# S5 stage of a two-layer decoder kernel: layer norm inside the turning matmuls, 32-row state matmuls side by side, feature-major readout, late row normalising

## The reference, cut to what matters

```python
h = _layernorm(DEEPNORM_ALPHA * h + _swiglu(...) + ple, ln2_g[0], ln2_b[0])     # layer 0 ends
...
bu = jnp.einsum('bsgc,gpc->bsgp', u, B_bar)            # u = h in 128 groups of 16 channels, 64 complex states each
_, states = lax.associative_scan(combine, (a, bu), axis=1)   # x[t] = A_bar * x[t-1] + bu[t]
y = jnp.einsum('bsgp,gcp->bsgc', states, C_mat).real.reshape(B, S, D)
y = y + d_skip * h
z = jax.nn.gelu(y)
val, gate = jnp.split(z @ w_glu, 2, axis=-1)
mix = val * jax.nn.sigmoid(gate)
...
h = _layernorm(DEEPNORM_ALPHA * h + mix, ln1_g[1], ln1_b[1])
```

## Time and profile before

| | us |
|---|---|
| median of 3 runs | 2477.44 (2476.77 to 2480.57) |
| the profiled execution | 2475.3 |
| span of the profiled execution, first to last instruction | 2473.5 |
| PE busy over the span | 2339.3 (95%) |
| first MATMUL of the S5 stage (L580) | at 1276.5 |
| first MATMUL of glu (L352) | at 1430.1 |

### The profile page before, as it was taken

The page is one execution under the profiler, slowest core; times in us unless marked ns, Lnnn a source line. Parts: engine busy times, 40 slices in busy tenths (PEclk is TensorE's granted clock), DMA queues, the critical chain, the costliest instruction groups (busy, mean ns, idle before and its releaser), DMA issues.

```text
span 2473.5 us, 32913 instructions
## 1 busy us (share of the span) xinstructions
PE 2339.3 (95%) x10996; PEld 1926.3 (78%) x10996; DVE 1456.8 (59%) x1906; ACT 1033.1 (42%) x1134; POOL 245.7 (10%) x345
## 2 busy tenths in 40 slices
PE   8999899999999999999948499989999999999996
PEld 6888687888888888888835488778888888888885
DVE  5544757666667776557846755475455444444555
ACT  4443544444444334443333054344444443344432
POOL 0000038501111011101230000010000000000001
PEclk9998999999999999999969799999999999999998
DMA  6554254767787667757684156556555565555553
GB/s 236 184 182 127 89 198 144 234 223 257 257 266 251 226 231 242 238 195 256 226 203 162 51 183 195 170 187 195 189 189 191 187 190 194 194 188 188 190 191 111
DMA packets 136991, 483.01 MB, mean 195 GB/s; under 512 B 18656, under 2 KB 19168, under 8 KB 135744
## 3 DMA queue, kind: packets, MB, share of 16 engines
q1 hardware_dynamic: 121568, 429.44, 53.5%
q0 software_dynamic: 14048, 50.80, 6.7%
q10 hardware_dynamic: 1280, 1.48, 0.2%
HBM read 457.80 MB, written 19.14 MB: 193 GB/s over the span
## 4 chain that ended last, share of the span: by engine, by line
PE 91%; DVE 5%; DMA 2%; issue 1%; ACT 1%; DVEq 0%; SPq 0%; ACTq 0%
PE ps L352 28%; PE ps L354 28%; PE ps L353 28%; PE ps L592 1%; PE ps L368 1%; PE ps L631 1%; DVE res L1205 1%; DMA raw<-in_w_in 1%; DVE w_lo L977 1%; DVE gated L1547 1%; DVE res L1207 1%; DMA h_quarter<-res 1%; DVE gated L1545 1%; DMA raw<-in_w_glu 0%; ACT w_hi L692 0%
## 5 line engine op out<-in xcount | busy, mean ns | idle before, releaser
L977 DVE TENSOR_TENSOR w_lo<-raw,w_hi 128x1024 fp32r<-128x1024 f32 (+1 forms) x782 | 953.5, 1222 | 861.3 <-ACT w_hi L692 855.4
L692 ACT ACTIVATE w_hi<-raw 128x1024 fp32r<-128x1024 f32 (+1 forms) x782 | 822.1, 1053 | 1190.0 <-PE ps L354 1157.9
L352 PE MATMUL ps<-w_hi,x_hi 128*128 128x512 f32 (+1 forms) x2336 | 917.3, 393 | 17.8 <-DVE x_lo L985 14.2
L354 PE MATMUL ps<-w_hi,x_lo 128*128 128x512 f32 (+1 forms) x2336 | 911.2, 390 | 0.0
L353 PE MATMUL ps<-w_lo,x_hi 128*128 128x512 f32 (+1 forms) x2336 | 910.8, 390 | 0.0
L352 PEld LDWEIGHTS ps<-w_hi,x_hi 128*128 128x128 f32 x2336 | 443.0, 190 | 109.5 <-DVE x_lo L985 16.1
L354 PEld LDWEIGHTS ps<-w_hi,x_lo 128*128 128x128 f32 x2336 | 442.9, 190 | 91.5
L353 PEld LDWEIGHTS ps<-w_lo,x_hi 128*128 128x128 f32 x2336 | 443.2, 190 | 88.6
L352 PE MATMUL ps<-w_hi,hid_hi 128*128 128x512 f32 x704 | 275.2, 391 | 0.0
L353 PE MATMUL ps<-w_lo,hid_hi 128*128 128x512 f32 x704 | 274.1, 389 | 0.0
L354 PE MATMUL ps<-w_hi,hid_lo 128*128 128x512 f32 x704 | 274.0, 389 | 0.0
(11 more groups left out here) (201 smaller groups left out, 1378.6 us busy)
## 6 DMA issues: line engine op xcount, KB each, us to landing
raw<-in_w_inA SPq DMA_DIRECT2D x192, 512.0 KB, 4.2
raw<-in_w_inB SPq DMA_DIRECT2D x160, 512.0 KB, 4.2
raw<-in_w_outA SPq DMA_DIRECT2D x96, 512.0 KB, 4.3
raw<-in_w_outB SPq DMA_DIRECT2D x80, 512.0 KB, 4.3
raw<-in_w_in SPq DMA_DIRECT2D x64, 512.0 KB, 4.0
raw<-in_w_gate SPq DMA_DIRECT2D x64, 512.0 KB, 4.3
raw<-in_w_glu SPq DMA_DIRECT2D x64, 512.0 KB, 4.2
raw<-in_w_out SPq DMA_DIRECT2D x32, 512.0 KB, 4.3
```

The source lines that it names most:

```text
L352: pe.matmul(o, hi[:, kt + k, cols], WH[:, s, k, 0:width], start=(kt + k == 0), stop=False)
L354: last = pe.matmul(o, lo[:, kt + k, cols], WH[:, s, k, 0:width], start=False, stop=(kt + k == depth - 1))
L692: act.activation(WH[:, s, :, 0:width], RAW[:, s, :, 0:width], ACT.Copy).then_inc(hi_ready, 1)
L977: dve.tensor_tensor(WL[:, s, :, 0:width], RAW[:, s, :, 0:width], WH[:, s, :, 0:width].bitcast(F32), ALU.subtract).then_inc(lo_ready, 1)
```

## The change

It touches the S5 stage, what is laid ready for it, and the normalising of RES.

- DVE makes two scaled and step-permuted identities: DQ (1/sigma of each token on the diagonal) and DC (-mean/sigma). PE multiplies RES, not yet normalised, by DQ: this turns tokens x features to features x tokens and applies 1/sigma. ONES times DC gives the shift. ACT makes gain and bias of it (CG), DVE adds both while copying to UT. The SBUF copies, `by_pairs`, U4, the Toeplitz table and POOL's clearing and 16 DMAs go.
- Input: 32 rows (a) of a feature tile against a 32 x 128 table, 32 matmuls a tile with 64 moving columns, straight into states-on-partitions form; the transposes back and e_slots go. Each of the four a has its own PSUM bank.
- Response in the block: 16 matmuls a tile of 32 x 32, row group a to column group a, started when half 0 of the scan has done 44 steps.
- Readout: 32 matmuls a tile, K = 128, 32 stationary columns of the table, the states (every 128th element of ST) moving, 64 columns; output features x tokens, so GELU goes to Z and straight to XH and XL without transposes.
- Scan: `lag` 9 in place of 17.
- Eight input tables are loaded during `outB0`, eight behind the first glu chunks; 16 slots in place of 10; glu chunks 4 to 7 behind the readout tables.
- RES is normalised by DVE alone during glu (`norm_late`, 16 instructions); `load_gb(2)` waits for it.
- `input_matrix` takes B without its fourfold copy, loaded in 8 smaller DMAs in place of 5.

```diff
+            def out_with_tables():
+                nb, per, c0, _ = PHASES["outB0"]
+                for j in range(nb * per):
+                    load(t["w_outB0"], j, c0 + j, 0, None, WB)
+                    if j == RING:
+                        sp.wait_ge(w_used, c0)
+                        sp.wait_ge(e_stored[0], 16 * 11)
+                        sp.wait_ge(e_stored[1], 16 * 5)
+                    if j >= 8 and j % 4 == 0:
+                        input_table(j // 4 - 2)
...
-                glu_chunks(RING, 2 * RING - 1)
-                sp.wait_ge(w_used, PHASES["glu"][2])
-                for q4 in range(4):
-                    quarter_normed(sp, 4 + q4 + 1)
...
-                        sp.dma_start(HQ[q4 % 2][32 * q:32 * q + 32, :, :], RES[:, q, cols]).then_inc(h4_in[q4 % 2], 16)
...
+                for tile in range(8, KT):
                     input_table(tile)
                 for n in range(KT):
+                    sp.wait_ge(e_done, n + 1)
+                    sp.dma_start(TS[n][:], c_dram[tile_of(n)].rearrange("p (a c n) -> p a c n", a=4, c=2)).then_inc(ts_in[n], 16)
+                glu_chunks(RING, 2 * RING)
...
+            def turn_u(kt):
+                for q in range(TT):
+                    last = pe.matmul(by_step(kt // 2 % 7, kt % 2, q), RES[:, q, P * tile_of(kt):P * (tile_of(kt) + 1)],
+                                     DQ[:, q, :].rearrange("p (s n) -> p s n", s=SUB), start=True, stop=True)
...
+            pe.wait_ge(u_ready, KT)
+            for kt in range(KT):
+                pe.wait_ge(ts_in[kt], 16)
...
+                for ri in range(2):
+                    for s in range(SUB):
+                        for a in range(4):
+                            rows = slice(PW * a, PW * (a + 1))
+                            last = pe.matmul(PS[:, 4 * (kt % 2) + a, SLOTS * ri:SLOTS * (ri + 1)], TS[kt][rows, s, ri, :],
+                                             UT[rows, kt, s, :], start=(s == 0), stop=(s == SUB - 1))
+                last.then_inc(e_done, 1)
...
+            pe.wait_ge(scan[0], 3 * 44)
+            for kt in range(KT):
+                for lag in range(SUB):
                     for a in range(4):
...
+                        pe.matmul(outputs(kt, a, lag, SUB), KTAB[rows, tile_of(kt), lag, :],
+                                  UT[rows, kt, 0:SUB - lag, :].rearrange("p s n -> p (s n)"),
+                                  start=(kt % 2 == 0 and lag == 0), stop=False, skip_group_check=True)
+            def read_out(kt):
+                pe.wait_ge(ts_in[kt], 32)
+                for s in range(SUB):
                     for ri in range(2):
+                        for a in range(4):
+                            last = pe.matmul(outputs(kt, a, s, s + 1), TS[kt][:, a, ri, PW * s:PW * (s + 1)],
+                                             ST[:, :, ri, 4 * kt + a], start=False, stop=(ri == 1), skip_group_check=True)
                 last.then_inc(y_done, 1)
...
+                act.activation(CG[:, kt % 2], PS[:, 7, 0:TOK], ACT.Identity, bias=GC[:, 1, tile_of(kt):tile_of(kt) + 1],
+                               scale=GC[:, 0, tile_of(kt):tile_of(kt) + 1]).then_inc(shift_ready, 1)
...
-            for q4 in range(4):
-                norm_quarter(1, q4)
...
+                dve.scalar_tensor_tensor(UT[:, kt].rearrange("p s n -> p (s n)"), PS[:, kt // 2 % 7, o:o + TOK],
+                                         GC[:, 0, tile_of(kt):tile_of(kt) + 1], CG[:, kt % 2], ALU.mult, ALU.add).then_inc(u_ready, 1)
...
-            steps, lag = SLOTS - 2, 17
+            steps, lag = SLOTS - 2, 9
...
+                    if k == 0 and j >= 4:
+                        norm_late(j - 4, 0)
+                    if k == 2 and j in (1, 2, 6, 7):
+                        norm_late((1, 2, 6, 7).index(j), 1, i)
...
-            pool.memset(KK[:], 0.0).then_inc(kk_zero, 1)
...
-                    pool.dma_start(KK[PW * s:PW * (s + 1), r::4, PW * s:P],
...
             pool.wait_ge(y_done, KT)
             pool.dma_start(PK[:], t["p"][1].rearrange("(t p) n -> p t n", p=P)).then_inc(p1_in, 16)
+            pool.wait_ge(ln_quarter, 8)
             load_gb(2)
```

More of the change, by code:

```diff
@@ L610, in _ @@
-            pe.wait_ge(e_out_act, 8)
-            pe.wait_ge(e_out_dve, 8)
-            pe.wait_ge(kk_in, 16 * 16)
-            def bank_of(pair):
-                tile, a = pair // 4, pair % 4
-                half = SLOTS * (tile // 8)
-                return PS[half:half + SLOTS, tile % 8, P * a:P * (a + 1)]
-            for pair in range(PAIRS):
-                pe.matmul(bank_of(pair), U4[:, pair, :], KK[:, pair, :], start=(pair % 4 == 0), stop=False,
-                          skip_group_check=True)
@@ L624, in read_out, with by_step @@
-            def read_out(n_):
-                tile = n_
-                count = 16 * (n_ // 10 + 1) + (16 * (3 if n_ % 10 < 4 else 2) if n_ % 10 < 6 else 0)
-                pe.wait_ge(ts_in[n_ % 10], count)
-                for a in range(4):
-                    pair = 4 * tile + a
+            pe.wait_ge(ones_set, 1)
+            def by_step(bank, half, q):
+                o = PS[:, bank, TOK * half:TOK * (half + 1)]
+                return o.rearrange("p (s q n) -> p q s n", s=SUB, q=TT)[:, q]
@@ L633, in read_out @@
                 last.then_inc(y_done, 1)
-            def turn_z(b):
-                pe.wait_ge(z_act, b + 1)
-                for half in range(2):
-                    rows = slice(SLOTS * half, SLOTS * (half + 1))
-                    for s in range(SUB):
-                        o = TOK * half + SLOTS * s
-                        if half and s == 0:
-                            pe.wait_ge(z_half, b + 1)
-                        last = pe.transpose(PS[:, b, o:o + SLOTS], Z4[rows, b, P * s:P * (s + 1)], ID[rows, rows])
-                    last.then_inc(z_turned if half else z_half, 1)
@@ L933, in _ @@
             for b in range(8):
                 gelu(b)
-                if b >= 3:
-                    z_high(b - 3)
-            for b in range(5, 8):
                 z_high(b)
@@ L1562, in _ @@
                 scan_op(1, n_, 0)
-            with dve.Fori(0, (steps - lag - 1) // 11) as i:
-                for k in range(11):
+            with dve.Fori(0, (steps - lag - 1) // 13) as i:
+                for k in range(13):
                     for n_ in range(3):
-                        scan_op(0, n_, lag + 1 + k, 11, i)
-                        scan_op(1, n_, 1 + k, 11, i)
+                        scan_op(0, n_, lag + 1 + k, 13, i)
+                        scan_op(1, n_, 1 + k, 13, i)
             for k in range(steps - lag, steps):
@@ L1761, in load_input @@
             def load_input(tile, n):
[L1763 to L1766 removed]
+                for a in range(4):
+                    rows = slice(PW * a, PW * (a + 1))
+                    pair = 4 * tile + a
+                    src = coef_dram[pair:pair + 1, :].rearrange("a n -> (a n)").partition_broadcast(PW)
+                    pool.dma_start(EC[n][rows].rearrange("p s c n -> p (s c n)"), src).then_inc(e_raw[n], 16)
+                    pool.dma_start(EB[n][rows], t["s5_b"][0:PW, pair]).then_inc(e_raw[n], 16)
             def store_input(tile):
```

270 lines of the change are left out of this document (124 added, 146 removed).

## The result

The changed kernel takes 2502.14 us (median of 4 runs, 2500.69 to 2504.59) against 2477.11 (4 runs) for the kernel before: a ratio of 1.0101, 95% interval 1.0089 to 1.0113. It is 1.0% slower where 1.5% faster was forecast, 61 us off, and it came out outside the range. The profiled execution took 2500.69 us, its span is 2498.8.

What follows compares the result with a forecast made beforehand. The bound was taken to change four times across the 178.7 us S5 stage, PE holding 91% of the last-ending chain. Glu 36.4 us earlier gave 2438.9, plus 2.1 for the median 2441.0; own range 2432 to 2452, full range 2424 to 2468.

Steps and rivals of the forecast that it cites:

- Steps 1 and 2: End of outB0 and turning: outB0's end 2.6 us earlier, first turn at 1259.3, UT whole at 1270.5 instead of 1292.2.
- Step 3: Input matmuls: 1024 instructions at 27 ns in four row groups, 27.9 us, last copy at 1299.8 instead of 1336.65.
- Step 4: Scan on DVE: 53 double steps of 1.22, 64.3 us; half 0 done at 1364.1 instead of 1391.4.
- Step 5: In-block response: 17.1 us plus 2.6 for half clock, done at 1362.1, hidden beside the scan.
- Rival D: In-block response and readout: diagonal 32 x 32 matmuls go one at a time, +13 us, 2490; chance 0.04.
- Step 6: Readout: strided states at 28.7 ns an instruction in four lanes, 14.7 us a half, glu starts at 1393.7.
- Rival B: Readout: four strided readers share one slot, 53 ns an instruction, 54.6 us, gain only 11, 2466; chance 0.12.
- Rival C: New stage's weight load and matmul pairs: PE isn't fed, 63 ns a pair, +46 us, 2523; chance 0.11.
- Step 7: Edits taken at nothing: table loads inside outB0, norm_late and load_gb(2) during glu; 0 to +5 us.

Runs made afterwards that it cites:

- e2: Changed kernel plus fifteen unread 128 x 128 x 128 matmuls filling PE's gap between turning and input matmuls: 2491.39 us, ratio 1.0061.
- e3: Changed kernel with e2's gap filler and one unread 128 x 128 x 256 matmul ahead of each input tile: 2489.45 us, ratio 1.0052.
- e4: Changed kernel with half 1 of the scan starting 25 steps behind half 0 instead of 9: 2497.09 us, ratio 1.0079.
- e11: Changed kernel, readout loops turned so 16 instructions in a row use one column group, at steps of 1, 16, 64, 128 elements: 2516.25 us (one run).
- e8: Changed kernel with readout tiles reading other states' values at steps of 1, 2, 4 ... 128 elements of 4 bytes: 2472.41 us (one run).
- e1: Changed kernel with the readout reading 64 contiguous elements, values of other states: 2464.04 us, ratio 0.995.
- e10: Changed kernel with the states array in groups of 16, so the readout steps 16 elements, same values: 2467.68 us, ratio 0.9966.
- e9: Changed kernel with e10's layout, e3's filler matmuls and a scan lag of 17: 2444.42 us, ratio 0.9879.
- e5: Changed kernel with the states array laid out slots innermost: readout contiguous, DVE's scan stepped by 256 bytes: 2472.44 us, ratio 0.9988.
- e6: Changed kernel with e1's contiguous readout, e3's filler matmuls and a scan lag of 17: 2443.21 us, ratio 0.9876.

## Why the prediction failed, step by step

**Steps 1 and 2 held.** Forecast 1259.3 for the first turn, it came at 1259.7; the turned rows were due at 1270.5 and were whole at 1272.6. The chain shows ACT and DVE taking turns, a shift of 0.57 us and a u of 0.49, where I had 0.47 a tile for both: they ended not the 1.2 us behind PE that I took but 3.1, and that pause is the gap ahead of step 3.

**Step 3 failed in its clock.** Its 27 ns, its four row groups side by side and its weight loads in parallel are right: e2 shows 28 to 29 ns at PEclk 1.00. The step took full clock for granted and never said so; it costed the half clock in steps 2 and 5, at a restart, and not here. The stage ran at 0.51: 53.6 us where 27.9 stood, and the last copy came at 1327.3 where 1299.8 stood. The Trainium skill (TensorE: Matmul & The Clock Gate, What's actually happening) states that half clock is the default state and that activity releases it. The half clock behind the scan's long wait agrees with it (PEclk 0.50 for the response's first 4 us, then 1.00). The input stage doesn't: PE was busy for 52.10 of 52.10 us there and the clock stayed at 0.50. The pause of 3.1 us is shown as one cause (e2); that it falls again and stays down points at the work itself, which one denser matmul a tile mends (e3); what in this work does it stays open.

**Step 4 held, from a later start.** 53 double steps took 62.9 us, 1.19 each for 1.22 (53 times 1.22 is 64.7, not the 64.3 of the sum). Half 0 was done at 1390.2, 26.1 late, 25.4 of them from step 3. The lag of 9 was to cost 9.8 us and return 6.8. e4 bears out that it returns most of its cost: with sixteen steps more of lag half 0 was done 15 us earlier, and the wait for half 1 was 12.9 us longer. What the step didn't have is that PE would wait for half 1 at all, since DVE's half 1 stood still during the readout.

**Step 5 held.** The response took 19.5 us (19.7 forecast), at PEclk 0.50 for its first 4, and ended before half 0 of the scan. Rival D falls.

**Step 6 failed in its price.** I took 1.79 ns a column in each of four lanes, from weight loads that one reader makes at a step of 512 bytes, 28.7 ns an instruction. One reader does pay that (e11: 110 ns at the median start to start, 1.72 a column), but four at that step pay 60. The first stair, at 16 bytes, is the rule of the Trainium skill (SBUF — State Buffer, Door 1: The DMA port swizzle) on which the prediction drew, and e8 agrees with it: 15 ns at 8 bytes, 28 at 16. The second stair is what the step lacked: 43 ns at 128 bytes, 58 to 60 at 256 and 512.

**Rival B came nearest to the mechanism**, four strided readers sharing, at 53 ns for 60, and e11 shows the sharing; but B had them share at any stride, and at 64 bytes they don't (30 ns). It had a chance of 0.12 and came out at 2466, since it was priced with step 3 intact: with step 3's 26 us on top it would have given 2492. What it lacked besides is that readers on other engines share too: half 1 was taken as long scanned, and cost 5.0 us of wait. From half 0's end to glu I had 29.6 us and it took 66.7, 37.1 more.

**Rival C fell** as put, since no feed of 45 ns or more showed (e2: 29 ns over 483 instructions, e1: 27 over 1024). The Trainium skill (TensorE: Matmul & The Clock Gate, Wait — 56ns, not 53.3ns?) has about 62 ns a MATMUL where hardware decode is off. The matmuls of e1 and e2 came quicker than that; whether decode was on, no run tells. If e1's `issue` pauses are the feed, it isn't far off: 27 ns a pair is all that came.

**Step 7 held.** In 1140 to 1252 us ACT waits for PE alone, where the earlier trace rows had 8.5 us for DMA, and PE idles 0.6 us in all of glu's matmuls (here ACT's group of outB0, and PE's first of glu; L354 and L355 have 0.0):

```profile
L684 ACT ACTIVATE w_hi<-raw 128x1024 fp32r<-128x1024 f32 x39 | 41.4, 1063 | 68.7 <-PE ps L355 68.7
```

```profile
L353 PE MATMUL ps<-w_hi,x_hi 128*128 128x512 f32 x256 | 99.8, 390 | 0.6 <-DVE x_lo L1567 0.6
```

**The sum.** Late turning 2.1, input matmuls 25.4, the rest of the scan -1.4, readout 37.1: 63.2 us late at glu, less 1.5 behind it, is 61.7 against the profiled execution's forecast of 2438.9. Either fault alone would have been survived in part: with the clock mended by fillers and the step kept the kernel is at 2489 (e3), by the estimate above at 2477 if the clock cost nothing; with the step mended and the clock left it is at 2468 (e10), the upper end of my range. So step 6 weighs more in the sign, and the range was too narrow since its cases varied one step at a time.

## What to carry to other kernels

When a layout hands PE a stepped moving operand in several column groups at once, keep the step small (here a step of 64 bytes took 30 ns an instruction against 27 for contiguous operands with their pauses, 256 and 512 bytes took 58 to 60 and stalled ACT, and at 512 DVE too), and look for a layout that groups elements for both the writer and the reader before choosing one side. A stage of many small matmuls has to be priced at both clocks, and a pause of a few us ahead of it can be part of its price (filling one of 3.1 us gave 10.7 us). When two steps have unknown prices, the range must hold the case where both go wrong.

## What the runs showed that I had not expected

- PE's reads at a step of 512 bytes from four column groups all but stop the others: scan instructions from 0.29 to 3.9 us, z from 0.58 to 7.6, x_lo from 0.69 to 7.2 (13, 13 and 10 times). At 256 bytes z is held up too: in e8 it starts in tile 6 and isn't done when that tile ends, 3.4 us on. At 64 bytes (e9, e10) there is no hold-up, and one reader at 256 bytes (e11) causes none either.
- The granted clock fell in mid-stage with no PE pause above 0.53 us (e2, at 1287.2), it stayed at 0.50 for 52 us beside a PE that never paused (the changed kernel), and one larger matmul a tile kept it up (e3).
- DVE pays some 0.05 to 0.08 us an instruction of 64 or 128 elements for a step of 256 bytes (e5), nothing for runs of 16 elements (e9).
- Contiguous operands let matmuls start 14 ns apart, but over 1024 of them PE sat 10.7 us idle for `issue` (e1): 25 to 27 ns a pair of weight load and matmul (e6, e1) is the best pace kept over a half here, so a step of 16 (30 ns) costs little more.
